# Another order of TensorE's and ScalarE's work in the attention steps of a two-block transformer

## The reference

```
s = qk * D**-0.5; s = where(mask, s, NEG); m = max(s, sink)
pr = exp(s - m);  denom = pr.sum() + exp(sink - m)      # SWA; DSA has no sink
o = (pr / denom) @ v
x = layer_norm(ALPHA * x + concat(oa, ob) @ w_o)
```

```
k, v = split(memn @ wkv)     # memn is the normalized memory, wkv is 1024 x 2048, one for each layer
```

## Time and profile before

| what | value |
|---|---|
| median of 3 runs | 1656.75 us (1654.83 to 1658.98) |
| the profiled execution, its own time | 1657.95 us |
| its span, first to last instruction | 1656.2 us |
| TensorE busy (matmul) | 1539.2 us, 93% |
| VectorE busy | 1055.2 us, 64% |
| ScalarE busy | 716.3 us, 43% |
| mean granted TensorE clock | 0.959 of 2.4 GHz |
| four attention stages, from first score to first product of the mix projection | about 84.6 to 140.5, 429.2 to 485.2, 820.5 to 887.2, 1279.9 to 1347 us |

### The profile page before, as it was taken

One profiled execution on the slowest core, in us unless ns is written; L12 is line 12 of the kernel. 1 busy time (PEld: TensorE's weight loads), 2 busy tenths in 40 slices (PEclk: granted clock), 3 DMA queues, 4 the chain that ended last, 5 costly groups with the idle time before them and its releaser, 6 DMA issues.

```text
span 1656.2 us, 24186 instructions
## 1 busy us (share of the span) xinstructions
PE 1539.2 (93%) x9781; PEld 1372.2 (83%) x9781; DVE 1055.2 (64%) x1676; ACT 716.3 (43%) x1042; POOL 62.9 (4%) x58
## 2 busy tenths in 40 slices
PE   6799999999989999979899889999898998889997
PEld 5677899998777999968777769999788777789996
DVE  6786955467869654675266456676852554566767
ACT  4355333334553333424464244445443643434542
POOL 1100000000100000011000000000010000000000
PEclk9899999999999999989799889999997998999999
DMA  8533555655334655634425633556444247245551
GB/s 293 179 127 115 172 179 196 206 180 192 127 115 164 218 178 188 242 105 147 130 69 184 206 102 129 193 187 205 152 138 138 68 148 239 82 153 178 188 194 51
DMA packets 184690, 267.26 MB, mean 161 GB/s; under 512 B 7382, under 2 KB 139396, under 8 KB 184452
## 3 DMA queue, kind: packets, MB, share of 16 engines
q1 hardware_dynamic: 179684, 260.48, 47.5%
q10 hardware_dynamic: 4896, 5.25, 0.9%
HBM read 260.46 MB, written 5.24 MB: 160 GB/s over the span
## 4 chain that ended last, share of the span: by engine, by line
PE 71%; DVE 15%; ACT 4%; DVEq 3%; issue 3%; POOL 2%; DMA 1%; SPq 0%; ACTq 0%; POOLq 0%
PE psw L688 16%; PE psw L690 16%; PE psw L689 16%; PE psa L688 4%; PE psa L689 4%; PE psa L690 4%; DVE wlo L1499 4%; POOL rstd L2127 2%; PE psa L780 2%; PE psa L777 2%; DVE xtok L1531 1%; PE psw L1061 1%; PE psw L798 1%; DVE r L1882 1%; DVE sy L1587 1%
## 5 line engine op out<-in xcount | busy, mean ns | idle before, releaser
L1499 DVE TENSOR_TENSOR wlo<-raw,whi 128x2048 fp32r<-128x2048 f32 (+2 forms) x201 | 452.7, 2258 | 327.4 <-ACT whi L1169 327.1
L1169 ACT ACTIVATE whi<-raw 128x2048 fp32r<-128x2048 f32 (+2 forms) x201 | 379.5, 1890 | 338.9 <-PE psw L690 247.4
L688 PE MATMUL psw<-xhi,whi 128*128 128x256 f32 x1472 | 416.8, 283 | 2.6 <-ACT r L1359 1.4
L690 PE MATMUL psw<-xhi,wlo 128*128 128x256 f32 x1472 | 416.6, 283 | 0.0
L689 PE MATMUL psw<-xlo,whi 128*128 128x256 f32 x1472 | 416.6, 283 | 0.0
L688 PEld LDWEIGHTS psw<-xhi,whi 128*128 128x128 f32 x1472 | 282.3, 192 | 5.1 <-ACT r L1359 2.2
L689 PEld LDWEIGHTS psw<-xlo,whi 128*128 128x128 f32 x1472 | 282.3, 192 | 1.2
L690 PEld LDWEIGHTS psw<-xhi,wlo 128*128 128x128 f32 x1472 | 282.3, 192 | 0.0
L688 PE MATMUL psw<-whi,xhi 128*128 128x512 f32 (+3 forms) x472 | 184.9, 392 | 16.6 <-DVE wlo L1499 13.7
L689 PE MATMUL psw<-wlo,xhi 128*128 128x512 f32 (+3 forms) x472 | 181.7, 385 | 0.0
L690 PE MATMUL psw<-whi,xlo 128*128 128x512 f32 (+3 forms) x472 | 181.6, 385 | 0.0
(11 more groups left out here) (261 smaller groups left out, 1959.4 us busy)
## 6 DMA issues: line engine op xcount, KB each, us to landing
raw<-in_w_gu SPq DMA_DIRECT2D x44, 1024.0 KB, 5.1
raw<-in_ffn_w_up SPq DMA_DIRECT2D x42, 1024.0 KB, 5.1
raw<-in_w_down SPq DMA_DIRECT2D x22, 1024.0 KB, 4.8
raw<-in_ffn_w_down SPq DMA_DIRECT2D x22, 1024.0 KB, 4.9
raw<-in_w_in SPq DMA_DIRECT2D x20, 1024.0 KB, 5.5
raw<-in_xa_wkv SPq DMA_DIRECT2D x16, 1024.0 KB, 5.5
raw<-in_w_o SPq DMA_DIRECT2D x8, 1024.0 KB, 5.0
raw<-in_w_out SPq DMA_DIRECT2D x8, 1024.0 KB, 5.3
```

The costliest lines, as they stand in the source:

```text
L688: pe.matmul(o, lh, rh, start=first, stop=False)
L690: return pe.matmul(o, ll, rh, start=False, stop=last)
L1169: nc.scalar.activation(tile_flat("hi", i), tile_flat("raw", i), ACT.Copy).then_inc(hi_ready, 1)
L1499: v.tensor_tensor(tile_flat("lo", i), tile_flat("raw", i), tile_flat("hi", i).bitcast(F32), ALU.subtract).then_inc(lo_ready, 1)
```

## The change

It has three parts, which apply to all four attention stages.

1. TensorE's step is now S(i), V(i-3), T(i-2), M: the memory half goes from second to last.
2. ScalarE's step is now K of the slot of the step before, H, C(i-2), E(i), A: copies come ahead of the exponentials, K one step later than before, and the weight split A (served behind the same half as before) with it, one step later and behind E.
3. ScalarE no longer waits for `kv_staged` and issues no store. SyncE issues the two stores of a memory tile just before the load that takes the tile's place in the ring, after the wait for TensorE to be done with the tile; it waits for `kv_staged` ahead of each.

VectorE's program is the same.

```diff
--- before.py
+++ after.py
@@ -642,6 +642,12 @@
                     sp.wait_ge(tile_done, max(e for e in extra if e < i) + 1)
                 elif i not in extra and raw_room(i):
                     sp.wait_ge(tile_done, raw_room(i))
+                if i not in extra and seq[i] >= NL and tiles[ring[seq[i] - NL]][0][1] == "kv":
+                    _, _, lm, k = tiles[ring[seq[i] - NL]][0]
+                    for n in (16 * lm + 2 * k, 16 * lm + 2 * k + 1):
+                        sp.wait_ge(kv_staged, n + 1)
+                        sp.dma_start(kv_halves[n], stage[lm][:, n % 2, :]
+                                     ).then_inc(kv_stored[n % 2], 16)
                 if key == (1, "d", 1, FS - 1):
                     sp.wait_ge(hid_ready, FS + 5)
                     sp.dma_start(rt[:], c["alibi"]).then_inc(alibi_loaded, 16)
@@ -798,9 +804,6 @@
                                 ins = pe.matmul(psw[:, 2 * (i % 2) + a, b * S:b * S + nk],
                                                 qT(kind, h, t), kT(kind, h, nk), start=True, stop=True)
                         ins.then_inc(scores_done, 1)
-                    n = memory_slot(block, l, i - first)
-                    if n is not None:
-                        memory_half(n)
                     if i - 3 >= first:
                         n = i - 3
                         u, hf = divmod(n, 2)
@@ -840,6 +843,9 @@
                                                soft[:, u % 2, h, kb * P:(kb + 1) * P], ident[:])
                             if q % 4 == 3:
                                 ins.then_inc(pt_done, 1)
+                    n = memory_slot(block, l, i - first)
+                    if n is not None:
+                        memory_half(n)
 
             def ffn(block, l, f0, norm_key, behind_up=lambda: None):
 
@@ -1235,13 +1241,31 @@
                 if n >= 2:
                     act.wait_ge(kv_stored[n % 2], 16 * (n // 2))
                 nc.scalar.activation(place, psa[:, 3, 0:TC], ACT.Copy).then_inc(kv_staged, 1)
-                act.wait_ge(kv_staged, n + 1)
-                act.dma_start(kv_halves[n], place).then_inc(kv_stored[n % 2], 16)
 
             def attention(block, l):
                 first = 2 * unit0(block, l)
                 count = 2 * sum(1 for x in units if x[0] == block and x[1] == l)
                 for i in range(first, first + count + 3):
+                    half = memory_slot(block, l, i - first - 1)
+                    if half is not None:
+                        memory_store(half, stage[block - 1][:, half % 2, :])
+                    if i - 3 >= first and i % 2 == 0:
+                        kind, t = units[(i - 3) // 2][2:]
+                        if kind != SLC:
+                            j = mix_part(kind, t)
+                            act.wait_ge(pv_done, i - 2)
+                            nc.scalar.activation(xhi[:, 2 * j - 2 * t:2 * j - 2 * t + 4, t * P:(t + 1) * P],
+                                                 psa[:, 2, :].rearrange("p (k s) -> p k s", k=4),
+                                                 ACT.Copy).then_inc(mix_hi, 1)
+                    if first <= i - 2 < first + count:
+                        n = i - 2
+                        for m in range(chunk0[n], chunk0[n + 1]):
+                            act.wait_ge(pt_done, m + 1)
+                            if m >= 4:
+
+                                owner = max(x for x in range(len(chunk0) - 1) if chunk0[x] <= m - 4)
+                                act.wait_ge(pv_done, owner + 1)
+                            nc.scalar.activation(pt[:, m % 4, :], psa[:, m % 2, :], ACT.Copy).then_inc(pt_ready, 1)
                     if i < first + count:
                         u, hf = divmod(i, 2)
                         kind, t = units[u][2:]
@@ -1258,26 +1282,6 @@
                                                            bias=nmx[:, u % 2, h:h + 1], scale=1.0,
                                                            accum_out=den[:, u % 2, h:h + 1])
                         ins.then_inc(exp_done, 1)
-                    half = memory_slot(block, l, i - first)
-                    if half is not None:
-                        memory_store(half, stage[block - 1][:, half % 2, :])
-                    if i - 3 >= first and i % 2 == 0:
-                        kind, t = units[(i - 3) // 2][2:]
-                        if kind != SLC:
-                            j = mix_part(kind, t)
-                            act.wait_ge(pv_done, i - 2)
-                            nc.scalar.activation(xhi[:, 2 * j - 2 * t:2 * j - 2 * t + 4, t * P:(t + 1) * P],
-                                                 psa[:, 2, :].rearrange("p (k s) -> p k s", k=4),
-                                                 ACT.Copy).then_inc(mix_hi, 1)
-                    if first <= i - 2 < first + count:
-                        n = i - 2
-                        for m in range(chunk0[n], chunk0[n + 1]):
-                            act.wait_ge(pt_done, m + 1)
-                            if m >= 4:
-
-                                owner = max(x for x in range(len(chunk0) - 1) if chunk0[x] <= m - 4)
-                                act.wait_ge(pv_done, owner + 1)
-                            nc.scalar.activation(pt[:, m % 4, :], psa[:, m % 2, :], ACT.Copy).then_inc(pt_ready, 1)
                     if half is not None and half % 2:
                         serve((2, "kv", half // 16, half // 2 % 8))
```

More of the change, by code:

```diff
@@ L1280, in attention @@
                             nc.scalar.activation(pt[:, m % 4, :], psa[:, m % 2, :], ACT.Copy).then_inc(pt_ready, 1)
+                    if i < first + count:
+                        u, hf = divmod(i, 2)
+                        kind, t = units[u][2:]
+                        nk = (t + 1) * P
+                        act.wait_ge(smax_done, i + 1)
+                        if kind == SWA:
+                            hs = esink[:, u % 2, 1, :].rearrange("p (a q) -> p a q", a=2)[:, :, 2 * hf:2 * hf + 2]
+                            nc.scalar.activation(hs, esink[:, u % 2, 0, :].rearrange(
+                                "p (a q) -> p a q", a=2)[:, :, 2 * hf:2 * hf + 2], ACT.Exp)
+                        for b in range(2):
+                            for a in range(2):
+                                h = a * 4 + hf * 2 + b
+                                ins = nc.scalar.activation(soft[:, u % 2, h, 0:nk], soft[:, u % 2, h, 0:nk], ACT.Exp,
+                                                           bias=nmx[:, u % 2, h:h + 1], scale=1.0,
+                                                           accum_out=den[:, u % 2, h:h + 1])
+                        ins.then_inc(exp_done, 1)
                     if half is not None and half % 2:
```

## The result

The changed kernel takes 1665.35 us (median of 5 runs, 1662.91 to 1665.78), the kernel before 1657.05 in 5 runs: ratio 1.0046, interval 1.0034 to 1.0058. It is 8.3 us slower (0.46%, clear of the noise), where 1665.3 was predicted. The profiled execution took 1665.35 us (span 1663.6).

The account below looks back on a forecast made before the run. The attention stages were taken as bounded by TensorE's own work, leaving only waits to change. 2 x 0.95 + 2 x 1.4 + 2 x 1.95 = +8.6 us took the median from 1656.75 to 1665.3 us; range 1655 to 1672.

Parts of the forecast that it names:

- Block 1, the moved items: Block 1 attention stages: late weight split leaves TensorE an uncovered 3.3 us wait; +0.95 us a stage, plus 1.4 for clock.
- Block 2: Block 2 attention stages: TensorE's waits total 4.6 us against 2.7 in the old order; +1.95 us a stage.
- I count no clock loss: Block 2 stages: TensorE's clock stays up through the new waits; with a 1.4 us loss, +3.35 a stage instead.
- The stores: SyncE's stores in the attention stages: issue and landing end within 3.0 us, inside the 4.7 available; counted as nothing.
- Rival (e): Stores land late behind weight loads, costing 1.6 us at six places in block 1; +18.2, 1675 us; chance 0.06.
- late pg load: Second pg tile's load leaves about 4 us later, hidden by the o stage's weight splits; uncovered it would cost 4 us.
- The zero for the 32 issues taken from ScalarE: Attention stages: removing eight store issues a stage saves ScalarE 3.2 us, but beside VectorE's wait, so gives nothing.
- The sum: Four attention stages together: +8.6 us, passed through whole to the kernel's time; median 1665.3 us.
- (a): Whole kernel goes as forecast: +8.6 us, 1664 to 1668, elsewhere given as 1662 to 1669; chance 0.50.
- (b): Attention stages: the clock doesn't fall in the new waits; +5.8 us or a little less, 1662.5; chance 0.20.
- (c): Attention stages: ScalarE's weight split isn't late, so VectorE finds it done; -2.6 us, 1654; chance 0.12.
- (d): Attention stages: old waits vanish and probabilities are ready 3.3 us earlier in block 1; -8.3 us, 1648.5; chance 0.07.

Follow-up runs that it names:

- e1: Changed kernel with ScalarE's weight split moved back ahead of the exponentials; 1655.49 us, ratio 0.9987 to the kernel before.
- e5: Changed kernel with one memory half per block 1 stage moved ahead of the turning of probabilities that waited; 1658.46 us, ratio 1.0004 to the kernel before.
- e9: The kernel before, unchanged, profiled once more; 1656.39 us, one run.
- e10: The changed kernel, unaltered, profiled once more; 1664.85 us, one run.
- e4: Changed kernel with six unused TensorE products filling the 3.2 us wait in each block 1 stage; 1664.41 us, ratio 1.0036 to the kernel before.
- e2: Kernel before with only the stores moved to SyncE, both old orders kept; 1654.38 us, ratio 0.9975 to the kernel before.
- e3: Changed kernel with the stores put back on ScalarE, both new orders kept; 1669.00 us, ratio 1.0065 to the kernel before.
- e8: Different TensorE and ScalarE orders of the same items, stores on SyncE, VectorE as before; 1645.49 us, ratio 0.9928 to the kernel before.
- e6: Kernel before with TensorE's new order alone, ScalarE's order and stores as before; 1715.44 us, ratio 1.0335 to the kernel before.

## Why the prediction was right

**Block 1, the moved items: right.** V4's wait went. B5 waited 2.49 us for A5 (2.6 forecast), X7 did not move (129.65 against 129.80), and T6 waited 3.16 us (3.3 forecast) with M7 behind it. That A's place is a cause, e1 shows by taking the loss away; e5 shows that M7's place behind T6 is the other half of it, as the forecast had it ("with nothing to cover it"). Before T6 TensorE fell behind the old order by 1.6 us (S7 at 41.4 us into the stage, before at 39.8), with a wait of 1.6 for L4 among its waits. That cost nothing, since T6 waited for P6 anyway. The forecast didn't name the wait, though its layout had V3 at 120.5 (120.31 measured). The stages of 58.9 and 59.2 us lie over the 57 to 58.5 that it gave, by the clock.

Rows and terms close in the first stage: 0.95, less 0.15 (T6 started that much earlier than forecast), less 0.15 (from T6 to the end 8.36 us at full clock, 8.5 forecast), plus 2.3 is 2.95, and the first stage was 3.0 longer.

**Block 2: the number was right, its parts were not.** Forecast +1.95 a stage, measured +2.25 and +2.1 (+1.7 and +2.3 from e9 to e10). T7 waited 1.71 (1.6 forecast) and B3 3.62 (4.0). But TensorE's waits in the first stage add up to 3.7 us, 1.0 more than before, where 4.6 were forecast; the rest is slow clock. "I count no clock loss" was the step that failed. From S10 (870.68) to M5 (874.96) TensorE ran for 4.11 us (4.28 less the wait of 0.17), and at the durations of the earlier trace rows S, V, T would take 1.10 + 0.59 + 1.03 = 2.72: 1.4 us of slow clock. How much of it was paid, e4 and e5 show, whose block 2 is the changed kernel's. In its first stage the clock stayed up there behind the same wait; from e4:

```profile
867.20 0.66 PE L846 MATMUL psa<-ident,sy 128*128 128x128 f32 x4 [1.71 <-DVE sy L1629]
...
870.44 1.09 PE L846 MATMUL psa<-ident,sy 128*128 128x128 f32 x8 [0.82 <-DVE sy L1629]
```

T8 waits 0.82 us instead of 0.17 (0.8 was forecast), and T7 to M5 takes 4.17 instead of 4.86. So half of the 1.4 lay where TensorE would have waited, and 0.7 was paid. That it nearly equals the waits that were forecast and didn't come is luck.

**The stores: harmless, and somewhat better than nothing.** Rival (e) is out: the stores landed in 1.8 us (median) and no wait for one shows. The Trainium skill ("DMA: Bandwidth & Descriptors", Two DMAs through the same engine are not ordered) has descriptors of one queue start in order; no run here shows a store held up behind a load by it. The late pg load was hidden, as forecast. The zero for the 32 issues taken from ScalarE was low in the old order: e2 gives 2.0 us of stage time and 3.2 by the medians. In the new order e3 gives 1.2 and 3.1, but there the cause isn't shown.

**The sum.** The stages gave +10.6 us (+9.9 in e9 and e10) for a forecast of +8.6; the 2.0 is block 1 (0.65 and 0.9, where the clock cost 0.9 and 1.1 more than forecast and the rest a little less) and the third and fourth stages (0.3 + 0.15). The median moved by 8.3, because the profiled executions of after spend 1407.3 us outside the stages and those of before 1408.6 and 1410.5. Most of that lies between the third and fourth stage, and it isn't fixed for before: 392.7 us in one execution and 390.3 in the other, 388.2 in both of after; behind the fourth stage it is after that takes longer, 310.7 against 309.1. Whether the change has a part in it stays open. That the median agrees with 1665.3 to 0.1 us is luck; by its own stages it would have been about 1667. The prediction also gives two ranges for (a): its terms, +7.2 to +11.4, make 1664 to 1668, and the 1662 to 1669 further down has no working.

**The other rivals.** (b) is out in block 1: the clock fell in both stages. (c), the split isn't late, is what e1 makes by another way, and its sizes held: the kernel 1655.5 against 1654, T6's wait 0.77 (0.8 forecast), block 1's stages 1.7 us shorter than before (1.6 forecast), block 2's +0.3 and 0 (0.3 forecast). In the changed kernel itself A5 started at 125.52 and B5 waited, so (c) is out. (d) would have needed P6 3.3 us earlier; it was 0.15 earlier.

## What to carry to other kernels

In queues that run in order, ask of a moved item what stands behind it in its own queue: here the copies went ahead of the exponentials and gained 2.7 us for VectorE's remainder, and a weight split that stayed behind them lost it again one instruction later. A long independent item (a memory half) is worth most directly before the instruction that will wait, and least directly behind it; and a wait left uncovered costs its own length and can cost the slow clock of what follows, more in one execution than in another. When two queues feed each other, try their orders in pairs: alone they cost 57 and 49 us here, together 8, and the pair in e8 gained 12 (the stores on SyncE included in all but the 57).

## What the runs showed of the hardware

- The clock: after 3.16 us without a product the granted clock was 0.50, and the next two items, 4.5 us of work at full clock, took 1.7 to 2.8 us more (after, e10); six useless products in the same gap kept it at 1.00 (e4). The length of a shorter wait alone didn't decide it: behind one of 2.2 us the clock fell in before and stayed up in e9, the same kernel; behind one of 1.71 us it fell in after and e10, for some 1.4 us, and stayed up in block 2's first stage of e4 and e5. The Trainium skill ("TensorE: Matmul & The Clock Gate", What's actually happening) has the slow clock as the default that activity lifts; that useless products kept the clock up agrees.
- The same 128 KB store landed 1.7 to 1.8 us after its issue (median of a group) when SyncE issued it (after, e2), and 2.6 to 3.7 us when ScalarE did (before, e3, e6). What makes the difference was not tested.
